# Half-height score products paired across heads, a third pair after half a panel, two weight splits moved and the forget products spread

## The chip, the cores and the metric

The kernel runs on one core of one Trainium2 chip. The metric is the device time of one execution in microseconds (us). The engines are named as the profile names them: PE (TensorE, the matrix products), PEld (its weight loads), DVE (VectorE), ACT (ScalarE), POOL (GpSimd) and SP (SyncE, which issues the DMAs).

## What is computed

The reference takes 256 tokens of width 1024 in fp32 through two stacks.

```python
for l in range(2):                        # first stack
    x = layer_norm(DN_ALPHA * x + 0.5 * swiglu(x, ffn1...))
    x = layer_norm(DN_ALPHA * x + hybrid_mixer(x, ...))
    x = layer_norm(DN_ALPHA * x + 0.5 * swiglu(x, ffn2...))
for l in range(2):                        # second stack
    h = rmsnorm(x);  x = x + merged(attention, convolution, pooling of h) @ w_o
    h = rmsnorm(x);  x = x + (silu(gt) * up) @ w_ffn_out
```

The hybrid mixer has three attentions of 8 heads with 64 channels each: A (a mixture of dilated patterns), B (a band of 128 keys with sinks) and C (64 keys per query, chosen by the score of an indexer with 8 more heads). The second stack has one attention, D, of 8 heads, with a forget gate per token and head: its logits get the difference of running sums of the log of sigmoid(x @ w_f), where w_f has 8 columns.

## The kernel before, in words

**Phases.** The work is a list of phases, `ffn, mix1, ffn` twice and `mix2, ffn` twice. Each engine has its own program that walks this list; the order inside a phase is written out by hand for each engine (`pe_mix1` L1036, `act_mix1` L1178, `pool_mix1` L1264, `dve_mix1` L1376 and the same four for `mix2`), and semaphores join them. Engines work strictly in that order: an instruction that waits holds up all that stands behind it.

**Weights.** They come from HBM in chunks of 128 x 2048 numbers (1 MB). A chunk lands in one of three raw buffers, ACT copies it to `w_hi` rounded to fp32r (`act_split`, L380 to L384), DVE writes the rest to `w_lo` (`dve_split`, L412 to L416), and each product of fp32 numbers is made of three fp32r products (`three`, L419). `act_split` waits until the chunk three places before in the ring has been used, `dve_split` until ACT is done, and the load of a chunk (`sp_chunk`, L364) until the split of the chunk three before it.

**Panels.** In a mixer the input projection is cut into panels of 512 columns. A panel takes two chunks (panel i of the first 13 takes chunks 2i and 2i+1), one for each half of the 1024 input channels. `panel_part` (L917) makes one half for one tile of 128 tokens, 12 products of 512 columns; `panel` makes the four parts, 48 products. Panels alternate between two pairs of PSUM banks, bankA and bankO0/1.

**Small jobs.** Between the panels stand jobs of attention, each in one of four other PSUM banks, taken in turn (`Mixer.small`, `take`, L899): transposes of the rotated queries and keys (`rope`), scores, transposes of the probabilities (`pT`), products with the values (`pv`), transposes of the outputs (`oT`). A job waits until the job four places before it has been read out of its bank (`w_free`).

**Scores.** The 16 score blocks (8 heads by 2 tiles of queries) are made in six units of at most one bank:

```python
UNITS = [(0, (0, 2, 4, 6)), (0, (1, 3, 5, 7)), (1, (0, 2)), (1, (1, 3)), (1, (4, 6)), (1, (5, 7))]
```

The first number is the tile of queries, the second the heads. Even heads lie on partitions 0 to 63 and odd heads on 64 to 127, so that a score product uses the upper or the lower half of the array's rows. A fp32 score product is two entries in the trace (L1060). In `mix2` (L1684 to L1694) each head has a score product (L1691) and one that adds the running sums of the keys (L1693). The units come one after the other, with no other work between. DVE scales, masks and reduces each unit to its row maxima (`logits`, L1443, L1922), ACT takes the exponentials (`exps`, L1134), and PE goes on with `values` (L939): four transposes for each unit, then the products with the values, which wait until ACT has copied the transposed probabilities to `pT` (`p_transposed`, L1152). For the indexer ACT applies a relu to each unit (L1205) into one of two buffers and DVE adds the heads up (`index_sums`, L1398).

**Order around the change.** In `mix1` PE goes: panels 0 to 2 with the transposes of ropes 0 and 1, the first quarter of panel 3, index scores, the rest of panel 3, rope 2, panel 4, rope 3, panel 5, scores B, panel 6, rope 4, values B, panel 7, rope 5, the outputs of B, scores C, panel 8, values C, panel 9, the outputs of C, scores A, panel 10, values A, panel 11. ACT goes, from the indexer on: six relus, the splits of chunks 8 and 9, the copy of panel 3 to `q_raw`, and so on; before values C it has `exps("C")`, the splits of chunks 18 and 19, `gate(8, 1)` and `p_transposed("C")`, and in the same way for A with chunks 22 and 23 and `gate(10, 3)`. POOL makes each rope from `q_raw` in four operations for each tile. In `mix2` PE goes: panels 0 and 1, the transposes of the keys of tile 0, the forget products (`forget_product`, L1613: 32 products of 16 and 8 columns), the keys of tile 1, panel 2, the queries, the running sums, channel panel 3 (96 products of 256 columns), scores D, channel panel 4, panel 5, values D.

Of the kernel before, what the change touches and what calls it, by code (L numbers as in the profile page):

```python
# [98 lines left out]
def build_program(nc, d, out):  # L99
    with ExitStack() as ctx:  # L100
# [10 lines left out]
        A = [bank("bankA0"), bank("bankA1")]  # L111
# [741 lines left out]
        jobs2 = [("qk", 0, 0), ("f",), ("qk", 0, 1)] + [("qk", 1, t) for t in range(TT)] + [("c",), ("cT",)]  # L853
# [49 lines left out]
        def pe_common(pe, M, ph, l, ml):  # L903
# [29 lines left out]

            def panel(i, n=PANEL):
                for h in range(2):
                    for tok in range(TT):
                        panel_part(i, h, tok, n=n)
# [95 lines left out]
            return take, freed, panel, panel_part, values, o_transposes, branch, merged_transposes, out_products  # L1033

        def pe_mix1(pe, ph, l):
            g = G[ph]  # L1036
            M = M1
            (take, freed, panel, panel_part, values, o_transposes, branch, merged_transposes,
# [11 lines left out]
            def scores(kind, n):  # L1050

                for u, (tile, heads) in enumerate(UNITS):
                    b, dst = take((kind, u) if n is None else (kind, n, u))
                    keys = P * (tile + 1)
                    for at, h in enumerate(heads):
                        half = slice(64 * (h % 2), 64 * (h % 2) + 64)
                        q = qi_T if n is None else Q_OF[n]
                        k = {None: kx_T[half, 3, 0:keys], "C": kx_T[half, 2, 0:keys],
                             "B": kx_T[half, h // 4, 0:keys], "A": ka_T[half, h // 2, 0:keys]}[n]
                        mm = pe.matmul(dst[:, at * keys:(at + 1) * keys],  # L1060
                                       q[half, h // 2, tile * P:(tile + 1) * P], k, start=True, stop=True)
                    mm.then_inc(M.w_ready[b], 1)
# [10 lines left out]
            scores("index", None)  # L1073
            panel_part(3, 0, 1)
            panel_part(3, 1, 0)
# [6 lines left out]
            scores("score", "B")  # L1082
            panel(6)
# [5 lines left out]
            scores("score", "C")  # L1089
            panel(8)  # L1090
# [4 lines left out]
            scores("score", "A")  # L1095
            panel(10)
# [83 lines left out]
        def act_mix1(act, ph, l, prefetch):  # L1180
# [19 lines left out]
            for u in range(6):  # L1200
                b, src = ready(("index", u))
# [4 lines left out]
            splits(4)  # L1206
            to_q_raw(3)
            splits(5)
# [1077 lines left out]
```

## Time and profile before

| | |
|---|---|
| median of the runs shown | 2047.75 us (2047.52, 2047.75, 2048.79) |
| the profiled execution, whole | 2049.36 us |
| its span, first to last instruction | 2047.4 us |
| PE busy | 2023.3 us, 99% of the span |
| DVE, ACT, POOL busy | 1233.5, 903.4, 273.3 us |
| mean granted TensorE clock | 0.997 |

The profiled execution lies 1.6 us above the median; 2.0 us of it lie outside the span. A busy PE is not yet a PE at its best: products are pipelined, so the distance between starts, not the length of a product, says how fast they go. Lines such as L421 to L423 are those of `three`; their tiles tell which product it is.

### The profile page before, as it was taken

To read this page: it belongs to the slowest core of one execution; us is meant where nothing else is said; L and a number is where in the kernel's file an instruction comes from. 1 tells how busy PE (TensorE), PEld (TensorE's weight loads), DVE (VectorE), ACT (ScalarE), POOL (GpSimd) and SP (SyncE) were. 2 spreads that over 40 slices of the span, in tenths; PEclk is the share of its full clock that TensorE was granted. 3 is DMA by queue.
4 is the path that set the end of the run, shared out by engine and by line. 5 is a ranking of instruction groups with operands and counts; after the bars stand their busy time and mean duration, and the time that the engine had idled before them with its cause. 6 is when DMAs were issued, how large, how long until landed. Compare 5 with 4: busy or idle time off the path is not lost.

```text
span 2047.4 us, 31170 instructions
## 1 busy us (share of the span) xinstructions
PE 2023.3 (99%) x12476; PEld 1807.8 (88%) x12476; DVE 1233.5 (60%) x1240; ACT 903.4 (44%) x1017; POOL 273.3 (13%) x209
## 2 busy tenths in 40 slices
PE   8999999999999999999999999999999999999999
PEld 7998888889998999878888998898899989888998
DVE  5557685475557555686467557565655566476554
ACT  4444445543444444355543444454444444544442
POOL 0000760010000000651010000323100021240000
PEclk9999999999999999999999999999999999999999
DMA  7655443456565556433365564545565553455553
GB/s 266 198 190 176 134 156 122 167 183 205 184 200 191 185 184 204 161 128 120 128 229 190 185 200 149 172 141 180 169 206 184 187 191 124 163 189 177 186 187 110
DMA packets 249122, 358.33 MB, mean 175 GB/s; under 512 B 24640, under 2 KB 164544, under 8 KB 249024
## 3 DMA queue, kind: packets, MB, share of 16 engines
q1 hardware_dynamic: 248880, 356.85, 53.0%
q8 instruction: 71, 1.16, 0.2%
q14 instruction: 27, 0.22, 0.0%
q10 hardware_dynamic: 144, 0.10, 0.0%
HBM read 355.85 MB, written 1.05 MB: 174 GB/s over the span
## 4 chain that ended last, share of the span: by engine, by line
PE 90%; DVE 5%; ACT 2%; POOL 1%; DMA 1%; issue 1%; SPq 1%; ACTq 0%; DVEq 0%; POOLq 0%
PE bankA L421 16%; PE bankA L423 16%; PE bankA L422 16%; PE bankO L421 12%; PE bankO L422 12%; PE bankO L423 12%; PE bankO L962 1%; DVE w_lo L415 1%; PE bankT L962 1%; PE bankT L447 1%; DVE bias_c L1409 1%; DMA w_raw<-in_w_ffn_in_dram 1%; POOL rope_out L1287 1%; DVE S_sb L1455 1%; DVE nmax L1460 1%
## 5 line engine op out<-in xcount | busy, mean ns | idle before, releaser
L415 DVE TENSOR_TENSOR w_lo<-w_raw,w_hi 128x2048 fp32r<-128x2048 f32 (+2 forms) x297 | 692.2, 2338 | 388.8 <-ACT w_hi L384 388.6
L384 ACT ACTIVATE w_hi<-w_raw 128x2048 fp32r<-128x2048 f32 (+2 forms) x297 | 563.1, 1900 | 458.4 <-PE bankA L423 317.7
L421 PE MATMUL bankA<-xT_hi,w_hi 128*128 128x256 f32 x1888 | 534.7, 283 | 0.0
L423 PE MATMUL bankA<-xT_hi,w_lo 128*128 128x256 f32 x1888 | 534.3, 283 | 0.0
L422 PE MATMUL bankA<-xT_lo,w_hi 128*128 128x256 f32 x1888 | 534.3, 283 | 0.0
L421 PEld LDWEIGHTS bankA<-xT_hi,w_hi 128*128 128x128 f32 x1888 | 362.2, 192 | 3.1 <-issue 0.7
L422 PEld LDWEIGHTS bankA<-xT_lo,w_hi 128*128 128x128 f32 x1888 | 362.2, 192 | 2.4
L423 PEld LDWEIGHTS bankA<-xT_hi,w_lo 128*128 128x128 f32 x1888 | 362.2, 192 | 0.0
L421 PE MATMUL bankO<-w_hi,xT_hi 128*128 128x512 f32 x432 | 173.0, 400 | 1.6 <-DVE w_lo L410 1.5
L423 PE MATMUL bankO<-w_hi,xT_lo 128*128 128x512 f32 x432 | 169.5, 392 | 0.0
L422 PE MATMUL bankO<-w_lo,xT_hi 128*128 128x512 f32 x432 | 169.2, 392 | 0.0
L421 PE MATMUL bankA<-w_hi,xT_hi 128*128 128x512 f32 (+1 forms) x384 | 154.0, 401 | 3.5 <-DVE w_lo L415 2.7
L800 POOL TENSOR_TENSOR rstd<-var_eps,minus_half 128x1 f32<-128x1 f32 x20 | 14.0, 702 | 1047.9 <-DVE var_eps L782 804.1
L423 PE MATMUL bankA<-w_hi,xT_lo 128*128 128x512 f32 (+1 forms) x384 | 150.9, 393 | 0.0
L422 PE MATMUL bankA<-w_lo,xT_hi 128*128 128x512 f32 (+1 forms) x384 | 150.8, 393 | 0.0
L421 PE MATMUL bankO<-w_hi,hT_hi 128*128 128x512 f32 x336 | 131.2, 391 | 0.0
L422 PE MATMUL bankO<-w_lo,hT_hi 128*128 128x512 f32 x336 | 131.2, 391 | 0.0
L423 PE MATMUL bankO<-w_hi,hT_lo 128*128 128x512 f32 x336 | 130.7, 389 | 0.0
L645 ACT ACTIVATE hT_hi<-h_sb 128x512 fp32r<-128x512 f32 x48 | 30.5, 636 | 185.5 <-PE bankO L423 185.5
L421 PEld LDWEIGHTS bankO<-w_hi,xT_hi 128*128 128x128 f32 x432 | 81.7, 189 | 19.9 <-DVE w_lo L410 2.6
L423 PEld LDWEIGHTS bankO<-w_hi,xT_lo 128*128 128x128 f32 x432 | 81.6, 189 | 17.7
L422 PEld LDWEIGHTS bankO<-w_lo,xT_hi 128*128 128x128 f32 x432 | 81.8, 189 | 15.8
(373 smaller groups left out, 3051.5 us busy)
## 6 DMA issues: line engine op xcount, KB each, us to landing
w_raw<-in_w_in_dram SPq DMA_DIRECT2D x184, 512.0 KB, 4.5
w_raw<-in_ffn_in_dram SPq DMA_DIRECT2D x172, 512.0 KB, 4.7
w_raw<-in_ffn_out_dram SPq DMA_DIRECT2D x88, 512.0 KB, 4.2
w_raw<-in_w_ffn_in_dram SPq DMA_DIRECT2D x88, 512.0 KB, 4.7
w_raw<-in_w_ffn_out_dram SPq DMA_DIRECT2D x44, 512.0 KB, 4.2
w_raw<-in_w_out_dram SPq DMA_DIRECT2D x16, 512.0 KB, 4.5
w_raw<-in_w_o_dram SPq DMA_DIRECT2D x16, 512.0 KB, 4.4
w_raw<-in_w_br_b_dram SPq DMA_DIRECT2D x8, 512.0 KB, 4.8
```

What stands on the lines that cost most here:

```text
L384: act.activation(cut(W_HI[slot(ph, i)], n), cut(w_raw[:, i % RING, :], n), ACT.Copy).then_inc(hi_done, 1)
L415: dve.tensor_tensor(cut(W_LO[slot(ph, i)], n), cut(w_raw[:, i % RING, :], n), cut(W_HI[slot(ph, i)], n).bitcast(F32), ALU.subtract).then_i ...
L421: pe.matmul(dst, hi, whi, start=start, stop=False, skip_group_check=True)
L422: pe.matmul(dst, hi, wlo, start=False, stop=False, skip_group_check=True)
L423: return pe.matmul(dst, lo, whi, start=False, stop=stop, skip_group_check=True)
L447: mm = pe.transpose(T[half][:, q * P:(q + 1) * P], buf[:, tok, kt * P:(kt + 1) * P], ident)
L645: act.activation(dst[:], h_sb[:].rearrange("p (t c) -> p t c", t=2), ACT.Copy).then_inc(hT_hi_done, 1)
L962: mm = pe.matmul(dst[:, h * 64:h * 64 + 64], pT[:, c:c + P], v, start=kk == 0, stop=kk == tile)
L1287: pool.tensor_tensor(outs[-1], src, c, ALU.mult).then_inc(rope_step, 1)
L1409: stepped(dve.scalar_tensor_tensor(acc, relu[:, u % 2, at * keys:(at + 1) * keys], misc[:, tile, 448 + h:449 + h], base, ALU.mult, ALU.add))
L1455: dve.scalar_tensor_tensor(s, src.rearrange("p (h k) -> p h k", k=keys), SCALE, m.unsqueeze(1).broadcast_to([P, len(heads), keys]), ALU.mu ...
L1460: red = dve.tensor_reduce(nm, s, AX, ALU.max, negate=True)
```

## The change

The score units are made in pairs, even and odd heads in turn, and the third pair (units 4 and 5) comes after half of the following panel. In `mix1` chunk 8 is split between the second and the third index unit and chunk 9 after the copy of panel 3 (ACT) or of rope 2 (DVE), and chunk 15 is split after `p_transposed("B")` and the copy of `va` (ACT) and after `normalise("B")` (DVE). In `mix2` the forget products are spread over panel 1, one pair behind each three products of 512 columns, and the key transposes come one quarter panel apart.

```diff
@@ PE, mix1
-            def scores(kind, n):
-                for u, (tile, heads) in enumerate(UNITS):
-                    b, dst = take((kind, u) if n is None else (kind, n, u))
...
+            def scores(kind, n, pairs):
+                for first in pairs:
+                    tile, evens = UNITS[first]
                     keys = P * (tile + 1)
+                    pair = [take((kind, u) if n is None else (kind, n, u)) for u in (first, first + 1)]
+                    for at in range(len(evens)):
+                        for parity, (b, dst) in enumerate(pair):
+                            h = evens[at] + parity
...
+                            mm = pe.matmul(dst[:, at * keys:(at + 1) * keys],
+                                           q[half, h // 2, tile * P:(tile + 1) * P], k, start=True, stop=True)
+                            if at == len(evens) - 1:
+                                mm.then_inc(M.w_ready[b], 1)
...
-            scores("index", None)
+            scores("index", None, (0, 2))
             panel_part(3, 0, 1)
+            scores("index", None, (4,))
             panel_part(3, 1, 0)
...
-            scores("score", "B")
-            panel(6)
+            scores("score", "B", (0, 2))
+            panel_half(6, 0)
+            scores("score", "B", (4,))
+            panel_half(6, 1)
...
-            scores("score", "C")
-            panel(8)
+            scores("score", "C", (0, 2))
+            panel_half(8, 0)
+            scores("score", "C", (4,))
+            panel_half(8, 1)
...
-            scores("score", "A")
-            panel(10)
+            scores("score", "A", (0, 2))
+            panel_half(10, 0)
+            scores("score", "A", (4,))
+            panel_half(10, 1)
@@ ACT, mix1
             for u in range(6):
+                if u == 2:
+                    act_split(act, ph, g, 8)
                 b, src = ready(("index", u))
...
-            splits(4)
             to_q_raw(3)
+            act_split(act, ph, g, 9)
             splits(5)
...
             exps("B")
-            act_split(act, ph, g, 15)
             p_transposed("B")
             for tok in range(TT):
                 panel_wait(6, tok)
                 act.activation(va[:, tok, :], A[tok][:, :], ACT.Copy).then_inc(M.m_free[0][tok], 1)
+            act_split(act, ph, g, 15)
@@ DVE, mix1
                 for u, (tile, heads) in enumerate(UNITS):
+                    if u == 2:
+                        dve_split(dve, ph, g, 8)
...
-            splits(4)
             rope_copy(2)
+            dve_split(dve, ph, g, 9)
...
             rope_copy(4)
+            normalise("B")
             dve_split(dve, ph, g, 15)
-            normalise("B")
@@ PE, mix2 (the ticket of job "f" also moves ahead of ("qk", 0, 0))
-            def forget_product():
+            def panel_and_forget(i):
                 b, dst = take(("f",))
                 pe.wait_ge(wf_lo_done, l + 1)
...
+                for h in range(2):
+                    for tok in range(TT):
+                        for t in range(4):
+                            panel_part(i, h, tok, t, 1)
+                            kt, c, tokens = 4 * h + t, 2 * tok * HEADS, slice(tok * P, (tok + 1) * P)
+                            pe.matmul(dst[:, c:c + 2 * HEADS], xT_hi[:, kt, tokens], wf[:, kt, :], ...)
+                            mm = pe.matmul(dst[:, c:c + HEADS], xT_lo[:, kt, tokens], wf[:, kt, 0:HEADS], ...)
...
+            def scores(pairs):
...
+                        for parity, (b, dst) in enumerate(pair):   # both score products, then both of the sums
...
-            panel(1)
+            panel_and_forget(1)
             qk_transposes(0, (0,))
-            forget_product()
+            panel_part(2, 0, 0)
             qk_transposes(0, (1,))
-            panel(2)
+            panel_part(2, 0, 1)
+            panel_half(2, 1)
             qk_transposes(1)
             running_sums()
             channel_panel(3)
             freed(("cT",))
-            scores()
-            channel_panel(4)
+            scores((0, 2))
+            channel_panel(4, (0,))
+            scores((4,))
+            channel_panel(4, (1,))
             panel(5)
```

## Rows read from the trace of the kernel before

**Rows 1.** The page, part 1: busy time, share and count of each engine.

```profile
PE 2023.3 (99%) x12476; PEld 1807.8 (88%) x12476; DVE 1233.5 (60%) x1240; ACT 903.4 (44%) x1017; POOL 273.3 (13%) x209
```

**Rows 2.** The waits of PE: engine, line, releaser, total us, times, longest us.

```profile
PE bankA L421 <- DVE w_lo L415: 2.7, 2, 1.4
PE bankT L962 <- ACT pT L1156: 1.7, 2, 0.9
PE bankO L1047 <- POOL rope_out L1300: 1.3, 2, 0.6
```

**Rows 3.** Windows: busy us of PE, PEld, DVE, ACT, POOL, granted clock, DMA, GB/s.

```profile
1302.00:1306.00 4.00, 4.00 (x36) 4.00 (x33) 2.32 (x5) 1.09 (x2) 3.04 (x3) 0.89 0.80 259
1306.00:1310.00 4.00, 4.00 (x13) 3.41 (x14) 1.47 (x6) 1.22 (x2) 3.84 (x4) 0.50 0.01 2
1310.00:1314.00 4.00, 4.00 (x15) 3.15 (x14) 2.02 (x3) 2.30 (x3) 2.07 (x2) 0.76 0.00 0
```

**Rows 4.** Timeline of PE, forget products: start, us, engine, line, tiles.

```profile
1302.10 0.26 PE L1620 MATMUL bankO<-wf,xT_hi 128*128 128x16 f32 x1
1302.21 0.25 PE L1622 MATMUL bankO<-wf,xT_lo 128*128 128x8 f32 x1
...
1305.55 0.35 PE L1622 MATMUL bankO<-wf,xT_lo 128*128 128x8 f32 x1
1305.76 0.36 PE L1620 MATMUL bankO<-wf,xT_hi 128*128 128x16 f32 x1
```

**Rows 5.** Timeline of PE, scores D of the first mix2.

```profile
1334.09 0.49 PE L1691 MATMUL bankT<-qc_T,qi_T 64*128 64x128 f32 x2
...
1335.53 0.27 PE L1691 MATMUL bankT<-qc_T,qi_T 64*128 64x128 f32 x1
1335.54 0.37 PE L1691 MATMUL bankO<-qc_T,qi_T 64*128 64x128 f32 x1
1335.64 0.27 PE L1691 MATMUL bankT<-qc_T,qi_T 64*128 64x128 f32 x1
...
1341.82 0.38 PE L421 MATMUL bankA<-xT_hi,w_hi 128*128 128x256 f32 x1
```

**Rows 6.** Timeline of PE, from scores C to values C, first mix1.

```profile
314.69 1.37 PE L1060 MATMUL bankT<-kx_T,qc_T 64*128 64x128 f32 x13
...
318.25 1.13 PE L1060 MATMUL bankT<-kx_T,qc_T 64*128 64x256 f32 x4 [0.19 <-DVE S_sb L1455]
319.31 0.50 PE L421 MATMUL bankA<-w_hi,xT_hi 128*128 128x512 f32 x1
...
330.35 1.03 PE L945 MATMUL bankO<-wide,S_sb 128*128 128x128 f32 x8
...
332.22 1.97 PE L962 MATMUL bankO<-misc,pT 128*128 128x64 f32 x16
```

**Rows 7.** Timeline of DVE and ACT in the same stretch.

```profile
321.48 0.68 DVE L1455 SCALAR_TENSOR_TENSOR S_sb<-bankT,bias_c 128x512 f32<-128x512 f32 x1
...
325.23 3.71 ACT L384 ACTIVATE w_hi<-w_raw 128x2048 fp32r<-128x2048 f32 x2
...
330.54 0.60 ACT L1168 ACTIVATE gates<-bankA 128x512 f32<-128x512 f32 x1 [1.13 <-PE bankA L423]
```

**Rows 8.** Timeline of PE and ACT, scores B to values B, first mix1.

```profile
276.48 1.37 PE L1060 MATMUL bankT<-kx_T,qb_T 64*128 64x128 f32 x13
...
292.71 1.90 ACT L384 ACTIVATE w_hi<-w_raw 128x2048 fp32r<-128x2048 f32 x1
...
295.67 1.97 PE L962 MATMUL bankT<-misc,pT 128*128 128x64 f32 x16 [0.85 <-ACT pT L1156]
```

**Rows 9.** Timeline of POOL, rope 3: its first and its last operation.

```profile
252.71 3.33 POOL L1287 TENSOR_TENSOR rope_out<-q_raw,cos 128x512 f32<-128x512 f32 x1 [8.65 <-ACT q_raw L1191]
...
263.59 1.27 POOL L1300 TENSOR_TENSOR rope_out<-rope_out,rope_tmp 128x512 f32<-128x512 f32 x1
```

**Rows 10.** Windows, columns as in rows 3: four us in the first mix2's entry.

```profile
1279.00:1283.00 4.00, 0.56 (x4) 0.14 (x3) 2.51 (x6) 3.18 (x5) 0.55 (x1) 1.00 0.16 10
```

More of the change, by code:

```diff
@@ L1031, in out_products @@
                 next_transposes(pe, ph, 1)
-            return take, freed, panel, panel_part, values, o_transposes, branch, merged_transposes, out_products
+            return take, freed, panel, panel_half, panel_part, values, o_transposes, branch, merged_transposes, out_products
         def pe_mix1(pe, ph, l):
@@ L1037, in pe_mix1 @@
             M = M1
-            (take, freed, panel, panel_part, values, o_transposes, branch, merged_transposes,
+            (take, freed, panel, panel_half, panel_part, values, o_transposes, branch, merged_transposes,
              out_products) = pe_common(pe, M, ph, l, l)
@@ L1600, in pe_mix2 @@
             ml = l + LAYERS
-            (take, freed, panel, panel_part, values, o_transposes, branch, merged_transposes,
+            (take, freed, panel, panel_half, panel_part, values, o_transposes, branch, merged_transposes,
              out_products) = pe_common(pe, M, ph, l, ml)
@@ L1638, in running_sums, with channel_panel @@
                           skip_group_check=True).then_inc(M.w_ready[b], 1)
-            def channel_panel(i):
-                for h in range(2):
+            def channel_panel(i, halves=(0, 1)):
+                for h in halves:
                     pe.wait_ge(lo_done, chunk_no(g, 2 * i + h) + RING)
@@ L1681, in conv_product @@
                         mm.then_inc(*((M.panel_ready, 1) if i == 11 or tok == 0 else (chunk_used, 1)))
-            def scores():
-                for u, (tile, heads) in enumerate(UNITS):
-                    b, dst = take(("score", "D", u))
+            def scores(pairs):
+                for first in pairs:
+                    tile, evens = UNITS[first]
                     keys = P * (tile + 1)
-                    for at, h in enumerate(heads):
-                        half = slice(64 * (h % 2), 64 * (h % 2) + 64)
-                        row = 64 * (h % 2) + h
-                        pe.matmul(dst[:, at * keys:(at + 1) * keys], q2_T[half, h // 2, tile * P:(tile + 1) * P],
-                                  k2_T[half, h // 2, 0:keys], start=True, stop=False)
-                        mm = pe.matmul(dst[:, at * keys:(at + 1) * keys],
-                                       ident[half, row:row + 1].broadcast_to([64, P]), neg_cT[half, 0:keys],
-                                       start=False, stop=True)
-                    mm.then_inc(M.w_ready[b], 1)
+                    pair = [take(("score", "D", u)) for u in (first, first + 1)]
+                    for at in range(len(evens)):
+                        c = slice(at * keys, (at + 1) * keys)
+                        for parity, (b, dst) in enumerate(pair):
+                            half = slice(64 * parity, 64 * parity + 64)
+                            pe.matmul(dst[:, c], q2_T[half, evens[at] // 2, tile * P:(tile + 1) * P],
+                                      k2_T[half, evens[at] // 2, 0:keys], start=True, stop=False)
+                        for parity, (b, dst) in enumerate(pair):
+                            half = slice(64 * parity, 64 * parity + 64)
+                            row = 65 * parity + evens[at]
+                            mm = pe.matmul(dst[:, c], ident[half, row:row + 1].broadcast_to([64, P]),
+                                           neg_cT[half, 0:keys], start=False, stop=True)
+                            if at == len(evens) - 1:
+                                mm.then_inc(M.w_ready[b], 1)
```

31 lines of the change are left out of this document (13 added, 18 removed).

## The prediction, on record before the changed kernel ran

> **What bounds the kernel now.** I read the page first, then the waits of PE, windows of the mixers, and the timeline of each engine around every edit. The page says PE: 2023.3 us busy, 99% of the span, no other engine above 60% [rows 1]. So time can come from three places only: PE's own work made shorter, PE's waits, and PE's clock. The table of waits shows how little stands in the second place, and that what there is belongs to this change [rows 2]: 1.4 us at most on chunk 8's split, twice, 0.9 us twice on ACT before values B, 0.6 us twice on POOL's rope. The windows show the third place [rows 3]: after the forget products the granted clock is 0.50 for the whole of one window and mixed in its neighbours.
>
> The profiled execution took 2049.36 us with a span of 2047.4; the median of the runs is 2047.75. I take gains worked out from the trace off the median. A difference of 0.2%, 4.1 us, is about what can be told from no change.
>
> **The change, part by part, for one layer of each mixer** (the second layer shows the same waits, so all is doubled at the end).
>
> *Forget products.* 32 products of 16 and 8 columns start 0.11 us apart (the first two of [rows 4]): 3.5 us in which PE does nothing wide. At the end of them the clock falls to the lower level, 1.2 GHz: the distance becomes 0.21 us (the last two of [rows 4]). How long it stays down comes from the windows: a mean of 0.89 over 4 us is 0.9 us at half clock, 0.50 is 4.0, 0.76 is 1.9, together 6.8 us [rows 3]. PE was busy throughout, so 3.4 us are lost. Spread, each pair stands behind three products of 512 columns. Its own cost is kept: a small product costs the 0.11 us of its weight load, which nothing 8 columns wide can hide, wherever it stands. So -3.4 us if the clock holds, 0 if it does not; I take -3.4, since PE was never at the lower level beside wide products. The price of the new order: panel 1 ends 3.5 us later, and POOL's work on the queries behind it. I follow that chain through DVE's reduction (now behind the key transpose) and POOL's four us a tile to the query transposes: it arrives within some 0.5 us of PE. I take +0.2, bounds 0 and +1.5.
>
> *Scores D.* From the first score product to the first of panel 4, 7.7 us [rows 5]. Units of unlike parity already overlap where they meet: bankT at 1335.53, bankO at 1335.54, the next bankT at 1335.64 [rows 5]. Two products on the two halves of the rows start 0.01 us apart and neither slows the other. Paired throughout, the first two units take 16 places of 0.11 us, 1.8 us, the others 8 places each of about 0.21 (two times the columns), 1.7 us a pair; with entries and exits between half-height and full-height products, of which there is now one more, 5.9 us. That is -1.8; bounds -0.8 (if PE cannot issue two weight loads and two products in 0.11 us for long; where the overlap shows, it lasts four places) and -1.9. Values D come after two panels, so ACT and DVE have room for the later third pair, and nothing takes it back.
>
> A rule speaks against this part. The Trainium skill (TensorEngine Tiling (Array Packing), Key Properties) says that changing the tiling mode drains the array. The row that bears on it: the last four products of scores C, 256 columns each, take 1.06 us up to the next full-height product [rows 6], where four places of 0.21 are 0.86. So a drain of 0.2 us on the way out, and as much on the way in by my estimate, stands in my sums; the change adds ten such excursions, 4 us in all, already counted.
>
> *Chunk 8.* PE no longer waits for its split, 1.5 us with what the wait's edges cost. But POOL's rope 3 is next. It runs from 252.71 to 264.86 [rows 9], started by ACT's copy of panel 3, and PE waits for it already [rows 2]. In the new order that copy comes when the last relu is done; DVE reaches it 2.3 us later because split 8 stands between its sums, and ACT saves the two splits of 3.7 us. I get the copy 1.05 us earlier, and rope 3 still crosses two DVE splits. So PE's gain, the shorter index scores included, is POOL's, -0.8; bounds -0.3 and -2.0.
>
> *Scores B and chunk 15.* The waits of scores on DVE (0.36 us and its edges) go, and split 15, 1.9 us of ACT ahead of the `pT` copies [rows 8], goes from PE's path. DVE's chain of six units and two splits stays, and then its copy of rope 4, which two of the transposes need. From the start of scores B to the first value product it was 19.2 us (276.48 to 295.67) [rows 8]; by that chain 18.0. So -1.2, bounds 0 and -1.7. Split 15 in its new place ends about 2.5 us before panel 7's second half needs it: nothing.
>
> *Scores C and A.* Here the edit turns against itself. Before, the scores took 4.6 us (314.69 to 319.31) [rows 6], and the value products began 17.5 us after the first score. Now: units 0 to 3 take 2.0 us, the half panel 5.5 (half of 319.31 to 330.35), and the third pair starts at 7.6 and is ready for DVE at 8.75. Before, DVE took unit 4 at 6.8 (321.48) and ACT's splits began at 10.5 (325.23) [rows 7]. All that follows is in ACT's order: exponentials, two splits of 3.7 us, two gate copies and two `pT` copies of about 0.55 us each. Begun 1.95 us later, and no longer waiting for PE (1.13 us [rows 7]), they reach the value products at 18.25. PE, which saved 1.4 us, is there at 15.95 and waits 2.3 us. Net +0.75 for C and the same for A, which has the same rows; bounds -1.4 (no wait at all) and +1.2.
>
> **Sum.** -3.4 + 0.2 - 1.8 - 0.8 - 1.2 + 1.5 = -5.5 a layer, -11.0 us in all: 2047.75 - 11.0 = 2036.8 us.
>
> **The rivals.**
>
> *The clock falls in a new place* (ends slower). The 2.3 us in which PE will stand before values C and A lie between 16 transposes of 1.75 us and small products of 6.2 us (332.22 up to the next panel). Nothing wide runs for ten us. Against it: before values B PE waited 0.85 us in such a stretch [rows 8] and kept its clock, and in the entry of mix2 it was busy 0.56 us in four and kept it [rows 10]. For it: that entry has 512-column products on both sides; the forget products, which did cost the clock, had not even a gap. There are four such places. A fall costs at least the 3.4 us that one costs now; if it covers the value products, each of which doubles as the forget products did (0.11 to 0.21), up to 6.2 us and some 2 more in the panel behind: 3.4 to 8. One fall: 2040 to 2045. Two give 2044 to 2053, three or four up to 2068. It decides from the point where falls cost over 11 us: two long or three short ones. For two or three at 6 us I write 2052.
>
> *The fall at the forget products stays*, because the transposes and the forget work together are still thin: 2043.6. Against it: three wide products to each pair.
>
> *Pairing does not pay*: PE issues too slowly, D gives 0.8 and the index pair nothing more: 2039 to 2041. The Trainium skill (TensorE: Matmul & The Clock Gate, the section on the 56 ns) has about 62 ns of issue for each product; by it a pair of places would take 0.124 instead of 0.11 us, and D would give 1.6 instead of 1.8. The trace cannot tell them apart in four places.
>
> *The waits at C and A do not come*, as ACT's work is quicker than I add up: then these parts give 1.4 each instead of costing 0.75, and the time is 2047.75 - 19.6, about 2028 to 2033.
>
> **How the numbers follow.** The sum as it stands, 2034 to 2040: 0.39, the likeliest. One fall in a new place: 0.14, of which 0.06 below 2043.65. Two or more: 0.32. The old fall stays: 0.04, half of it below. Pairing doesn't pay: 0.05. No waits: 0.06. Faster by over 0.2%: 0.39 + 0.06 + 0.02 + 0.05 + 0.06 = 0.58. Same: 0.10. Slower: 0.32, all of it the clock. Leaving out some 0.15 of the longest falls and a few hundredths of the lowest, the range is 2033 to 2056. Since both signs hold much: the likeliest case alone is 2034 to 2040.
>
> **What would show it.** In the changed profile: granted clock 1.00 through panel 1 and the key transposes of mix2, no row of products 0.21 us apart there; scores D some 5.9 us without the half panel between; no wait on L415 in panel 4 but one of 1 to 2 us on POOL's L1300 before rope 3's second tile; no wait of L1060 on DVE; waits of L962 on ACT's `pT` in C and A of about 2.3 us, four in all, and about 1 us before values B for DVE's copy of rope 4. I am wrong if the windows of values C and A show a clock of 0.5 in more than one place, or if those four waits are missing.

## The result, and the profile after

The changed kernel takes 2065.12 us in the median of four runs (2059.54 to 2066.23); the kernel before took 2047.85 beside it. The ratio is 1.0079, 95% interval 1.0064 to 1.0093: it is 17 us slower. The forecast said 2036.8 with a range up to 2056, so both the sign and the range were wrong. What happened is the first rival: PE's clock fell in new places.

The first two lines of the page (busy times before: [rows 1]):

```profile
span 2064.0 us, 31202 instructions
PE 2028.7 (98%) x12476; PEld 1808.6 (88%) x12476; DVE 1253.3 (61%) x1240; ACT 903.8 (44%) x1017; POOL 270.1 (13%) x209
```

PE has the same 12476 products as before, some of them now side by side, and yet it is busy 5.4 us longer, and the span is 16.6 us longer. So it stands 11.2 us more, and it is slower while it works. The waits of PE (who waited <- for whom: us in total, times, longest us), against [rows 2]:

```profile
PE bankO L965 <- ACT pT L1170: 8.5, 4, 2.1
...
PE bankO L948 <- DVE qi_T L1402: 4.9, 2, 2.7
PE bankA L421 <- DVE w_lo L415: 2.7, 2, 1.4
PE bankO L1066 <- DVE oT_loC L1367: 1.2, 2, 0.6
PE bankO L421 <- DVE w_lo L415: 1.0, 2, 0.5
```

The four waits on `pT` are those the prediction announced, 2.1 us each. The second row was announced as about 1 us and is 2.17 in the first layer and 2.73 in the second. The third stands in panel 4 where chunk 8's wait had been, but it is chunk 9's. The first, second, fourth and fifth row are new, 15.6 us; the 4.5 us that PE waited before values B, between the scores and for POOL are gone. That leaves the 11 us of standstill. The rest of the loss is clock. Windows of 4 us through values B and values A of the first layer (columns as in [rows 3]: busy us and count of PE, PEld, DVE, ACT, POOL, then the granted clock, DMA share and GB/s):

```profile
292.00:296.00 4.00, 1.83 (x16) 1.42 (x14) 3.97 (x6) 2.26 (x8) 3.92 (x5) 0.98 0.17 66
296.00:300.00 4.00, 4.00 (x20) 4.00 (x20) 0.90 (x3) 0.53 (x1) 3.77 (x4) 0.50 0.00 0
300.00:304.00 4.00, 4.00 (x22) 4.00 (x20) 0.23 (x2) 3.70 (x5) 0.00 (x0) 0.50 0.02 4
...
308.00:312.00 4.00, 4.00 (x16) 3.23 (x15) 4.00 (x3) 0.00 (x0) 0.00 (x0) 0.81 0.12 10
374.00:378.00 4.00, 1.88 (x17) 1.67 (x16) 4.00 (x2) 4.00 (x7) 0.00 (x0) 0.97 0.17 24
378.00:382.00 4.00, 4.00 (x21) 4.00 (x21) 0.75 (x3) 0.56 (x2) 0.00 (x0) 0.50 1.03 373
382.00:386.00 4.00, 4.00 (x27) 4.00 (x26) 0.54 (x2) 2.99 (x3) 0.00 (x0) 0.68 0.36 134
```

In both places a window in which PE was busy for 1.8 or 1.9 us of four comes first, and then PE, fully busy, runs at 0.50, that is at 1.2 GHz. The timeline of PE at values B shows the stop and what it costs behind it:

```profile
294.64 1.25 PE L948 MATMUL bankO<-wide,S_sb 128*128 128x128 f32 x8 [2.17 <-DVE qi_T L1402]
295.73 3.42 PE L965 MATMUL bankT<-misc,pT 128*128 128x64 f32 x16
298.95 1.06 PE L948 MATMUL bankT<-wide,S_sb 128*128 128x128 f32 x4
```

The first 16 products with the values (`pT` in the row) took 1.8 us up to the next transposes before (295.67 to 297.47); here they take 3.2 (295.73 to 298.95). Such falls lie at values B and A in the first layer, at values C and A in the second, and one more at the entry of the first mix2, where PE waits 3.48 us for `hn`; their sum is 44.4 us at half clock, so 22 us lost, against 6.8 before (13.7 us at half clock, both times at the forget products).

Stage by stage, from starts of products in the two traces (us, first and second layer, "after" in the same order; "pv" is the first product with the values; a forecast is for one layer):

| stage | before | forecast | after |
|---|---|---|---|
| index scores to scores B | 37.89, 37.85 | -0.8 | 37.72, 37.64 |
| scores B to pv B | 19.19, 19.19 | -1.2 | 19.42, 19.98 |
| pv B to scores C | 19.03, 19.03 | 0 | 25.71, 19.19 |
| scores C to pv C | 17.52, 17.51 | +0.75 | 18.89, 18.90 |
| pv C to scores A | 18.14, 18.14 | 0 | 18.15, 24.65 |
| scores A to pv A | 17.56, 17.56 | +0.75 | 19.20, 19.22 |
| pv A, first to last | 6.09, 6.10 | 0 | 9.36, 7.74 |
| mix2, entry to next phase | 196.2, 193.4 | -5.0 | 194.1, 187.8 |

The differences add up to 17.3 us, against 16.6 between the two spans; the other phases together took 0.7 us less. 18.1 of them are the four falls in the mixers (6.7, 6.5, 3.3 and 1.6 in the rows 3, 5 and 7 of the table), 6.9 are mix1 without the falls (the forecast for it was -1.0), and mix2, its entry's fall included, gave back 7.7.

What was forecast of mix2 came. A window over panel 1 with the forget products in it:

```profile
1318.00:1322.00 4.00, 4.00 (x24) 3.40 (x23) 2.42 (x5) 2.89 (x3) 3.20 (x3) 1.00 1.04 380
```

And scores D, against [rows 5]: PE's timeline at the start of the first two pairs, at the start of the third pair, and at the first panel product behind each.

```profile
1358.04 0.37 PE L1713 MATMUL bankT<-qc_T,qi_T 64*128 64x128 f32 x1
1358.05 0.37 PE L1713 MATMUL bankO<-qc_T,qi_T 64*128 64x128 f32 x1
...
1358.48 0.27 PE L1718 MATMUL bankT<-kx_T,wide 64*128 64x128 f32 x1
1358.49 0.27 PE L1718 MATMUL bankO<-kx_T,wide 64*128 64x128 f32 x1
1358.59 0.27 PE L1713 MATMUL bankT<-qc_T,qi_T 64*128 64x128 f32 x1
1358.60 0.27 PE L1713 MATMUL bankO<-qc_T,qi_T 64*128 64x128 f32 x1
...
1361.76 0.39 PE L421 MATMUL bankA<-xT_hi,w_hi 128*128 128x256 f32 x1
```
```profile
1367.70 0.48 PE L1713 MATMUL bankT<-qc_T,qi_T 64*128 64x256 f32 x1
...
1369.62 0.39 PE L421 MATMUL bankA<-xT_hi,w_hi 128*128 128x256 f32 x1
```

3.72 and 1.92 us, 5.64 together (forecast 5.9, before 7.73). Behind the first pair, which takes 0.21 us, two products of 128 columns share each 0.11 us all the way, so "pairing does not pay" is out. The Trainium skill (TensorE: Matmul & The Clock Gate, "Wait — 56ns, not 53.3ns?") has the 62 ns for each product only where hardware decode is off, a condition that the prediction left out; no run here shows which decode was at work. By that figure two products would have needed 0.124 us, and the trace has 0.11.

Why was the stop at values B so long? DVE's timeline of the changed kernel in the first layer, and POOL's beside it:

```profile
291.43 0.42 DVE L1455 TENSOR_SCALAR bias_c<-bias_c 128x128 f32<-128x128 f32 x2
291.77 2.22 DVE L1459 TENSOR_TENSOR bias_c<-bias_c,wide 128x128 f32<-128x128 f32 x2
293.91 1.27 DVE L1402 COPY qi_T<-bankO 128x512 f32<-128x512 f32 x2
```
```profile
291.64 1.33 POOL L1303 TENSOR_TENSOR rope_out<-q_raw,cos 128x512 f32<-128x512 f32 x1 [17.14 <-PE bankO L1050]
292.94 0.77 POOL L1307 TENSOR_TENSOR rope_tmp<-q_raw,sin 128x256 f32<-128x256 f32 x1
```

The same two additions of `chosen` (DVE's step that makes the mask of C) took 0.62 us in the kernel before:

```profile
291.93 0.62 DVE L1441 TENSOR_TENSOR bias_c<-bias_c,wide 128x128 f32<-128x128 f32 x2
```

POOL's rope 5 waits for PE's transposes of rope 4. PE reached them 1.5 us earlier (290.57 instead of 292.03) while DVE's chain hardly moved, and so POOL's first operations met DVE's additions. The copy of rope 4 stands behind them and the transposes of units 2 and 3 behind that. In the second layer it was a smaller one that they met: DVE's addition of 8 columns to `sinkm` (L1489, at 934.70) took 1.27 us instead of 0.17, beside POOL's first operation of 1.28 us (at 934.67), and the steps of `chosen` behind it were stretched too. The Trainium skill (SBUF — State Buffer, SBUF: two separate sides) says that a DVE operation with two SBUF inputs and a POOL operation that reads SBUF exclude each other for a whole instruction. The trace agrees: the first of the two additions took 1.36 us instead of 0.29 and ended at 293.13, behind the POOL operation that ended at 292.97, and the second took 0.94 instead of 0.42 beside POOL's next one of 0.77.

### The profile page after: what moved, and what is told of

Same layout as the page of the kernel before. It is cut to its first block, busy times and chain, and to the rows that moved or that the text cites. A ratio compares the mean times of both kernels' runs of the same rounds, so it can differ in the third digit from the quotient of the medians.

```text
span 2064.0 us, 31202 instructions
## 1 busy us (share of the span) xinstructions
PE 2028.7 (98%) x12476; PEld 1808.6 (88%) x12476; DVE 1253.3 (61%) x1240; ACT 903.8 (44%) x1017; POOL 270.1 (13%) x209
## 4 chain that ended last, share of the span: by engine, by line
PE 90%; DVE 6%; ACT 2%; issue 1%; DMA 1%; SPq 0%; POOL 0%; DVEq 0%; ACTq 0%
PE bankA L421 16%; PE bankA L423 16%; PE bankA L422 16%; PE bankO L421 12%; PE bankO L422 12%; PE bankO L423 12%; DVE w_lo L415 2%; PE bankO L965 2%; PE bankT L965 1%; DVE bias_c L1427 1%; PE bankT L447 1%; ACT w_hi L384 1%; DVE nmax L1478 1%; DMA w_raw<-in_w_ffn_in_dram 1%; DVE S_sb L1473 1%
## 5 line engine op out<-in xcount | busy, mean ns | idle before, releaser
L421 PE MATMUL bankO<-w_hi,xT_hi 128*128 128x512 f32 x432 | 177.2, 410 | 1.9 <-DVE w_lo L415 1.0
L423 PEld LDWEIGHTS bankO<-w_hi,xT_lo 128*128 128x128 f32 x432 | 82.3, 190 | 18.1
```

The lines of the kernel that those rows point to most:

```text
L421: pe.matmul(dst, hi, whi, start=start, stop=False, skip_group_check=True)
L423: return pe.matmul(dst, lo, whi, start=False, stop=stop, skip_group_check=True)
```

## The experiments

Twelve kernels ran, each beside the kernel before on the same chip; a ratio is that of its time to that kernel's. Diffs are against the changed kernel, but for e8 to e10 (against the kernel before) and e11, e12 (against e7). A fall below is a stretch of granted clock 0.50 among the value products.

**e1: whole panels for B, C and A.**

```diff
-            scores("score", "C", (0, 2))
-            panel_half(8, 0)
-            scores("score", "C", (4,))
-            panel_half(8, 1)
+            scores("score", "C", (0, 2, 4))
+            panel(8)
```

and the same for B (panel 6) and A (panel 10).

> The changed kernel with the third pair of units of B, C and A back beside the other two and the whole panel behind them; the alternation of parities, the moved splits and the spread forget products stay. Theory (the half panel delays ACT and DVE, PE then stands still among transposes and value products, and there the clock falls): the four waits of 2.12 us on pT go, no window of values A, B or C shows a clock of 0.5, and the time is 2047.85 - 6.8 (forget) - 3.6 (scores D) - 1.6 (chunk 8) - 1 to 3 (scores) = 2033 to 2035, or up to 3.4 more if the entry of mix2 still loses its clock. Rival 1 (the alternating score products themselves, denser and with more changes between half and full height, cost the clock): the falls stay, 2052 to 2062. Rival 2 (the falls are a matter of where each stretch happens to lie): some stay at other places, 2038 to 2050.

2037.74 us, ratio 0.9956 (0.9942 to 0.9970). No stop among the values and no fall there; the theory holds, and rival 1 (the alternation) is out. PE waits for DVE at the third pair instead:

```profile
PE bankT L1066 <- DVE S_sb L1467: 6.2, 6, 1.5
```

The entry of mix2 still lost its clock, which the expectation put at up to 3.4 us more.

**e2: whole panels for C and A only.** The e1 edit without B.

> Only C and A have their third pair back beside the others. Theory: the waits on pT go and with them the falls at values C and A, 23.9 us of half clock in the profiled run of the changed kernel, so 12 us, while the 1.4 us that the scores had gained by the half panel go back against the 2.1 us of each wait (-0.7 each, -2.8): 2065.1 - 12 - 2.8 = 2050. The fall at values B (13.65 us of half clock, 6.8 us) stays. Rival 1 (alternating products cost the clock): no change of the falls, about 2062. Rival 2 (placement): B's stretch of layer 2 may now fall as well, 2050 to 2057.

2048.43 us, ratio 1.0005 (0.9994 to 1.0017), near the theory's 2050: no wait on `pT`, no fall at C or A, the stops at B (2.17 and 2.73 us) as they were, with a fall in the first layer only in the profiled execution.

**e3: a whole panel for B only.** The e1 edit for B alone.

> Only B has its third pair back beside the others. Theory: DVE gets units 4 and 5 before the panel, its chain to the copy of rope 4 ends earlier, the 2.17 us stop of PE inside the transposes of values B goes and with it its fall (6.8 us): 2065.1 - 6.8 - 1 = 2057, the falls at C and A as before. Rival 1 (alternating products): 2064. Rival 3 (the stop comes from POOL's rope 5 beside DVE's chosen, whatever the scores do): the stop stays at 1.5 to 2.2 us and so does the fall, 2064.

2054.47 us, ratio 1.0039 (1.0023 to 1.0056): the stop at B is gone. Rival 3 had the collision right, but not "whatever the scores do": with the whole panel ahead of the transposes of rope 4, PE reaches them at 291.94 instead of 290.57, POOL starts at 293.02, and DVE's additions are through by then.

```profile
291.76 0.62 DVE L1457 TENSOR_TENSOR bias_c<-bias_c,wide 128x128 f32<-128x128 f32 x2
293.02 1.28 POOL L1301 TENSOR_TENSOR rope_out<-q_raw,cos 128x512 f32<-128x512 f32 x1 [18.50 <-PE bankO L1050]
```

The C and A stops were all there (8.5 us in four), yet in the profiled execution only those of the second layer cost the clock. Windows around values C of both layers, the same work at the same pace:

```profile
328.00:336.00 8.00, 5.88 (x50) 5.47 (x49) 5.41 (x5) 6.43 (x10) 0.00 (x0) 1.00 0.45 148
961.00:969.00 8.00, 5.88 (x43) 5.52 (x42) 5.41 (x5) 5.84 (x9) 0.00 (x0) 0.89 0.49 163
```

PE is busy 5.88 of 8 us in both; one keeps the clock and one doesn't. The twelve runs of this kernel reach from 2046.6 to 2068.2: whether a stop costs the clock is settled anew each time.

**e4: pT ahead of both splits.**

```diff
             exps("C")
+            p_transposed("C")
             splits(9)
             gate(8, 1)
-            p_transposed("C")
```

and the same for A.

> The half panels stay everywhere; ACT copies pT of C and of A before the splits of chunks 18, 19 and 22, 23 and the gates, not after them. Theory (it is the standstill that costs the clock): PE no longer waits 2.12 us four times (-8.5), the falls at C and A go (-12), the later splits are in time for panels 9 and 11: 2044 to 2046, with B's fall still there. Rival 4 (a long stretch without wide products costs the clock even without a gap): the waits go, the falls stay, 2056. Rival 5 (the splits become late instead): waits of L421 on w_lo in panels 9 and 11, 1 to 3 us each.

2058.18 us, ratio 1.0041 (1.0026 to 1.0057): far above the theory's 2045. The standstill was not taken away but moved, four times 1.34 us. Without a stop among the values, PE stops for the late split behind them:

```profile
342.85 0.59 PE L421 MATMUL bankO<-w_hi,xT_hi 128*128 128x512 f32 x1 [1.34 <-DVE w_lo L415]
```

```profile
342.00:346.00 4.00, 3.15 (x8) 2.47 (x9) 3.93 (x6) 3.03 (x4) 0.00 (x0) 0.64 0.51 140
```

Rival 5 came as written (1.34 us, four times), and in the first layer both of these stops came with a fall of 3.4 us. The other part of the miss is at values B: here the second layer fell too, for 17.1 us, where the changed kernel's profiled execution had kept its clock at the same stop. The experiment left open whether thin products alone would do (rival 4). e5 settles that.

**e5: one split on each side of pT.**

```diff
             exps("C")
-            splits(9)
-            gate(8, 1)
+            act_split(act, ph, g, 18)
             p_transposed("C")
+            act_split(act, ph, g, 19)
+            gate(8, 1)
```

and the same for A with chunks 22 and 23.

> The changed kernel; before values C and A ACT does only one of the two splits (18, 22) ahead of the copies of pT, the other split (19, 23) and the gate copies behind them. Theory (a standstill of PE, wherever it comes beside products of 64 columns, costs the clock; moving both splits behind, as before, only moved the standstill of 1.3 us to panels 9 and 11): ACT's exponentials end at 334.7 and one split takes 1.9 us, so pT is in time, and chunk 18 and 19 are in time for panel 9; no wait over 0.5 us at C and A, no fall there, 2065.1 - 8.5 - 12 = 2044 to 2047 with B's falls and the entry of mix2 left. Rival (thin products alone cost it): the falls at the end of values C and A stay, 3.4 us of half clock each as with both splits behind, 2048 to 2055.

2045.67 us, ratio 0.9993 (0.9982 to 1.0004). The waits on `pT` and the late splits at C and A are gone, and with them every fall there, though the row of thin products is as long as before. The falls at B remain, in both layers of the profiled execution (297 and 928 us). So this row of narrow products (some 8 us of transposes and value products) keeps the clock when nothing stops it.

**e6: copy of rope 4 ahead of the mask.**

```diff
+            rope_copy(4)
             chosen()
-            rope_copy(4)
```

> The changed kernel; DVE copies rope 4 before it makes the choice mask of C, not after it. Theory: the stop of PE inside the transposes of values B (2.17 and 2.7 us) goes, because it was the mask under POOL's rope 5 that was late and not the half panel, and B's fall goes with it: 2065.1 - 4.9 - 6.8 = 2053 to 2055; the four waits on pT and the falls at C and A stay. Rival: the stop becomes a wait on something behind the copy (the sinks' sums, ACT's pT) of 1 us or more and the fall stays, 2060 to 2064.

2054.09 us, ratio 1.0035 (1.0020 to 1.0051). The stops at B shrink to 0.28 and 0.79 us, and B keeps its clock; all four stops at C and A are followed by falls in the profiled execution.

**e7: all mends.** The edits of e5 and e6, and

```diff
-            rope_copy(2)
             dve_split(dve, ph, g, 9)
+            rope_copy(2)
```

> Both of these together, and chunk 9's DVE split before the copy of rope 2. Half panels, alternation, moved splits and spread forget products all stay. Theory: no stop over 1 us is left between the products of B, C and A, no fall but perhaps one at the entry of mix2: 2065.1 - 8.5 - 12 - 4.9 - 6.8 - 1.5 = 2031 to 2035, below the version with whole panels by what the scores' waits on DVE cost there (6.2 us). Rival (half panels thin the stretch by themselves): falls stay, 2037 to 2045, and whole panels are the better way.

2033.58 us (2031.45 to 2035.78), ratio 0.9938 (0.9924 to 0.9951): the theory's range, and faster than both kernels. Half panels, alternation, moved splits and spread forget products are all in it. Its busy times, three of its waits (that on POOL is the longest left in mix1) and two windows, over values B and values A:

```profile
PE 2009.8 (99%) x12476; PEld 1790.4 (88%) x12476; DVE 1253.1 (62%) x1240; ACT 903.3 (44%) x1017; POOL 270.0 (13%) x209
```
```profile
PE bankO L1050 <- POOL rope_out L1318: 2.0, 2, 1.0
PE bankO L1066 <- DVE oT_loC L1369: 1.2, 2, 0.6
PE bankO L948 <- DVE qi_T L1404: 0.8, 1, 0.8
```
```profile
296.00:300.00 4.00, 4.00 (x39) 4.00 (x38) 1.74 (x5) 3.48 (x5) 3.92 (x5) 1.00 0.01 4
...
368.00:372.00 4.00, 4.00 (x36) 3.92 (x35) 1.48 (x1) 4.00 (x6) 0.00 (x0) 1.00 0.60 224
```

**e8: the stop alone, in the kernel before.** ACT makes two copies into `q_raw`, which nobody reads any more in that layer, ahead of the copies of `pT` of C and of A.

```diff
+            act.wait_ge(rope_done, (l + 1) * (ROPES * TT))
+            for at in range(2):
+                act.activation(q_raw.rearrange("p t (r c) -> p (t r) c", r=4), ident.unsqueeze(1).broadcast_to([P, 8, P]), ACT.Copy).then_inc(dose_step, 1)
+                act.wait_ge(dose_step, 4 * l + 0 + at + 1)
             p_transposed("C")
```

and the same for A, with `4 * l + 2 + at + 1`.

> The kernel before, with two needless copies of 1024 columns on ACT (into a free buffer) ahead of the copies of pT of C and of A, about 1.0 us each: a standstill of PE of some 2 us at the same four places, but between two whole panels, with nothing else changed. Theory (the standstill costs the clock): 2047.85 + 4 x 2.1 = 2056 and falls at one to four of the places, 3.4 to 6.8 us of half clock each, 2058 to 2066. Rival (the standstill costs only itself; the half panel with the third pair in it, or the alternation, is needed for a fall): four waits of 2 us, no new fall, 2055 to 2057.

2062.73 us (2058.09 to 2068.81), ratio 1.0079 (1.0061 to 1.0096): the changed kernel's ratio, from the kernel before and four stops. The wait, and the clock behind three of the four:

```profile
333.62 1.97 PE L963 MATMUL bankO<-misc,pT 128*128 128x64 f32 x16 [2.14 <-ACT pT L1157]
```
```profile
338.00:342.00 4.00, 4.00 (x21) 4.00 (x20) 0.00 (x0) 1.52 (x1) 0.00 (x0) 0.50 0.00 0
...
380.00:384.00 4.00, 4.00 (x22) 4.00 (x20) 0.80 (x2) 2.99 (x3) 0.00 (x0) 0.50 0.01 2
...
980.00:984.00 4.00, 4.00 (x25) 4.00 (x25) 0.80 (x2) 1.22 (x3) 0.00 (x0) 0.60 0.50 178
```

Neither half panel nor alternation is needed. Four stops of 2.14 us are 8.6 us, and the kernel lost 15.5 (2047.24 beside it): the stop costs itself and, three times in four here, the clock.

**e9: only the forget products spread** (the whole `panel_and_forget` part of the change).

> The kernel before with only the forget products spread over panel 1 and the key transposes one quarter panel apart. Theory: the two falls of 6.8 us of half clock go, -3.4 each, and the new order costs nothing to see: 2047.5 - 6.8 = 2040 to 2041, with no product of the mixers at the lower clock. Rival: the chain of the queries behind the later panel 1 makes PE wait 1 us or more a layer, or the entry of mix2, which has lost its clock in every version with the changed mix1 and in none with the old one, loses it here too: 2042 to 2044.

2044.65 us, ratio 0.9986 (0.9977 to 0.9995), 3.2 us faster and not 6.8. The second mix2 gives the full sum: 193.4 us become 189.9. In the first, 196.2 became only 195.4: the fall at the forget products is gone, but the entry lost its clock here, which in the profiled execution of before it had kept [rows 10].

```profile
1279.00:1283.00 4.00, 0.53 (x3) 0.23 (x2) 2.51 (x5) 3.18 (x5) 0.55 (x1) 0.97 0.16 11
1283.00:1287.00 4.00, 4.00 (x16) 3.31 (x16) 1.07 (x2) 0.75 (x2) 0.00 (x0) 0.60 0.63 172
```

Nothing of the change lies ahead of that entry in this kernel, so its loss is no effect of mix1, although every version with the changed mix1 had lost it.

**e10: only scores D changed.**

> The kernel before with only scores D changed (alternation, third pair after half of channel panel 4). In the changed kernel the scores took 5.64 us against 7.73, so theory: -2.1 a layer, 2047.5 - 4.2 = 2043. Rival (the time gained there is lost again in a wait behind it, for values D): 2045 to 2047.5, with a new wait of L945 or L962 in mix2.

2044.15 us, ratio 0.9981 (0.9972 to 0.9990), the theory's 2043 to 1.2 us; no new wait before values D. In the profiled execution the entry of the first mix2 lost its clock here too.

**e11: the mended kernel with whole panels** (e7 with the edit of e1).

> The version with all mends (one split ahead of pT, copy of rope 4 first, chunk 9 ahead of the copy of rope 2), but with the third pair of B, C and A back beside the others and whole panels. Theory: with the falls gone the half panel is worth what the scores otherwise wait for DVE, 1.5 us at B and 0.8 at C and A (the waits of the version with whole panels), 3.1 a layer less 0.5 to 1 of waits that it causes before the values: 2033.6 + 4 to 6 = 2038 to 2040. Rival (the half panel never paid, and the mends carry the whole gain): 2033 to 2035.

2037.83 us, ratio 0.9954 (0.9940 to 0.9968), against 0.9938 of e7. The waits of the third pair on DVE are back at 6.2 us. The first mix1, from its first transposes to those of the next phase, takes 250.0 us here and 247.9 in e7, the second 249.8 and 248.3: the half panel is worth 2.1 and 1.5 us once it causes no stop.

**e12: the mended kernel without alternation.**

```diff
-                    pair = [take(("score", "D", u)) for u in (first, first + 1)]
-                    for at in range(len(evens)):
...
+                    for parity in range(2):
+                        b, dst = take(("score", "D", first + parity))
...
+                        for at in range(len(evens)):
```

and in the same way in mix1.

> The version with all mends, half panels kept, but the two units of a pair made one after the other everywhere, as before. Theory: alternation is worth 2.1 us a layer in D and some 0.4 in the index scores and up to 1.1, 0.4 and 0.4 in B, C and A, as far as the waits on DVE between the pairs don't swallow it: 2033.6 + 4.2 + 2 to 4.6 = 2040 to 2042. Rival (only D gains, as elsewhere DVE sets the pace): 2037.5 to 2039.

2039.89 us, ratio 0.9964 (0.9950 to 0.9978). The time lies between the theory's and the rival's, and the mechanism is the rival's: mix1 takes 248.1 and 248.3 us against 247.9 and 248.3 in e7, so there alternation is worth 0.2 us or nothing. Scores D carry the difference of 6.3 us between the two kernels: the first two pairs take 5.79 us and the third 2.90, against 3.72 and 1.92, so 3.05 in each of two layers.

```profile
1325.50 0.37 PE L1715 MATMUL bankT<-qc_T,qi_T 64*128 64x128 f32 x1
...
1331.29 0.38 PE L421 MATMUL bankA<-xT_hi,w_hi 128*128 128x256 f32 x1
...
1337.23 0.48 PE L1715 MATMUL bankT<-qc_T,qi_T 64*128 64x256 f32 x1
...
1340.13 0.39 PE L421 MATMUL bankA<-xT_hi,w_hi 128*128 128x256 f32 x1
```

8.69 us, while undivided and unalternated scores took 7.73, so dividing them costs 1.0 us. Nearly all of it is overlap: where units 3 and 4 met, in the kernel before, the last four products of the one and the first four of the other took 0.98 us side by side (1338.92 to 1339.90); divided, they take 0.96 (1330.33 to 1331.29) and 0.97 (1337.23 to 1338.20) one after the other.

```profile
1338.92 0.70 PE L1691 MATMUL bankT<-qc_T,qi_T 64*128 64x256 f32 x4
1339.90 0.38 PE L1691 MATMUL bankT<-qc_T,qi_T 64*128 64x256 f32 x1
```

**All profiled executions together.** There are 84 value stretches (B, C, A in two layers of 14 kernels, before and after included). The fall begins in the last 0.7 us of the stop or up to 2.2 us behind it:

| stop of PE in or right behind the stretch | stretches | with a fall |
|---|---|---|
| none, or up to 0.88 us | 56 | 0 |
| 1.34 us, behind it | 4 | 2 |
| 2.1 to 2.7 us, in it | 24 | 18 |

The entry of the first mix2, with its stop of 3.4 us, lost the clock in 12 of the 14, the second, which has no such stop, in none. Other stops of 0.9 us and more, all of them shorter than 2 us, never came with a fall: 22 of 1.31 to 1.38 us in panel 4 of mix1, between products of 512 columns; 6 of 1.52 us between score products, with a panel on both sides (e1, e3, e11); 6 of 0.95 to 1.06 us in the transposes of rope 3; 8 of 0.90 to 1.73 us at the entries of the phases behind mix2.

## Why the prediction was wrong

**The step that failed is the price of the stops before values C and A.** The sum has them as waits alone, "Net +0.75 for C and the same for A", and puts the clock at nothing; it went into a rival with a chance of 0.46. The waits came, at 2.12 us against 2.3 forecast. What the runs showed in place of "nothing" is that a stop of 2.1 to 2.7 us there comes with a fall in 18 of 24 stretches, and that the four falls in the mixers cost 18.1 us of the changed kernel. By that rate "no fall" at four such stops was the least likely outcome, and not the likeliest. The evidence set against it was a stop of 0.85 us before values B and a half-idle window at the entry of mix2. The first belongs to a class that never cost the clock (0 of 56, ten of them with a stop of 0.79 to 0.88 us), so it said nothing about stops of over 2 us. The second was one execution of an entry that loses its clock in 12 of 14. A row that "kept its clock" is one draw. The rival's own arithmetic was sound: "three or four up to 2068" holds what came, but the likeliest value was written down as 2052, and the range was cut at 2056, below the price worked out.

One reading of the rows leaned the wrong way as well: "PE was never at the lower level beside wide products". The fall of [rows 3] goes on beside them: the first products of 512 columns behind the forget products start 0.43 us apart (1307.52 and 1307.95 in the kernel before), against 0.23 at full clock. It began among narrow ones, and that much was right.

From the forecast to the result it is 28 us. Of these 18.1 are the four falls in the mixers, 3.4 the fall at the entry of the first mix2, 3.4 scores B, 3.1 scores C and A, and 1.2 chunk 8; the rest of mix2 gave 1.1 more than forecast.

**Scores B and chunk 15** was the second failure: -1.2 forecast, +0.2 and +0.8 measured, and it made a fifth and a sixth stop of over 2 us. "DVE's chain ... stays, and then its copy of rope 4" left out that the earlier transposes also release POOL, beside which the last pieces of that chain are stretched: the two additions took 2.22 us instead of 0.62. I had looked at what DVE waits for and not at what PE's gain would start. With the copy moved ahead (e6) the stage takes 17.4 and 18.0 us, the 18.0 forecast.

**Scores C and A**: +0.75 forecast, +1.4 and +1.65 measured. The waits were right to 0.2 us; I missed that the second pair now waits for DVE's copies out of the banks (0.34 us at C, 0.62 at A), so that the third pair started 8.2 us behind the first score instead of 7.6 (329.67 less 321.44), and 8.5 at A.

**Chunk 8**: -0.8 forecast, -0.2 measured. The wait on its split went, but the wait on POOL that I expected in its place did not come, because chunk 9's split, now beside rope 3, took 3.02 us and held PE 1.38 us; chunk 11's held it 0.5 us later. With split 9 ahead of the copy of rope 2 (e7) the stage gives 0.8 and 0.9 us, and the wait on POOL of 1.0 us appears as forecast.

**The forget products** were right: -3.6 us in the second mix2 against -3.4 + 0.2, no fall beside the wide products, no late query. **Scores D** were mis-sized by 0.3 us on the safe side, 5.64 for 5.9. The term is the passage between full and half height, 0.2 us each way in the sum. The changed kernel's rows give about 0.1 in (the first step is 0.21 us instead of 0.11, and 0.32 instead of 0.21 in the third pair) and 0.1 out (0.30 from 1369.32 to the panel, instead of 0.21).

**The whole**: with the stops mended the kernel takes 2033.6 us, ratio 0.9938, near the 2036.8 of the forecast. That nearness confirms little: e7 has three edits that the forecast kernel lacks, and it is the case of the prediction's last rival, no waits at C and A, for which it had 2028 to 2033. What stands is the price of the forget products and, within 0.3 us, of scores D; the parts of mix1 had waits left out, and the rival taken for a possible mishap decided the case.

## What to carry to other kernels

A long stop of PE is not priced by its length. Here one of 2.1 to 2.7 us among narrow products cost its length and, three times in four, the clock on top, up to 7.6 us of it (values B of e5, second layer: 46.8 us from scores B to scores C, where the changed kernel with the same stop and no fall took 39.2). One of 3.4 us between wide products cost the clock in 12 of 14. Stops under 0.9 us never did, and of those between 0.9 and 2 us only the ones right behind the value products (2 of 4). So before moving work, count the stops of 2 us and more that it creates, and those of over a microsecond beside narrow products, and take each as a likely fall; one clean pass in one trace is no proof against it. When PE comes earlier somewhere, follow also what its semaphores start on POOL, and move the copy that PE needs next ahead of whatever collides with it.

## What the runs showed of the hardware

- The same kernel keeps or loses the clock from one execution to the next at the same place with the same stop (e3's values C in the two layers; runs of e3 from 2046.6 to 2068.2 us), and the version without long value stops has a narrow spread (e7, five runs: 2031.45 to 2035.78). The kernel before, without them too, spread from 2043.8 to 2053.2 in 21 runs, so a wide spread alone does not point at them.
- The length of a fall varies as much: 3.4 to 17.1 us at half clock for a stop among the value products (3.4 for values A of the changed kernel's second layer, 13.7 for its values B), 3.4 or 6.8 at the entry of the first mix2, between products of 512 columns.
- Products of 128 columns on the two halves of the rows start in pairs every 0.11 us for 30 products on end (scores D, behind a first pair of 0.21 us), and those of 256 columns every 0.21 or 0.22, so the two halves do work side by side for as long as the program alternates.
- Divided scores without alternation cost 1.0 us more than undivided ones, but 0.86 of it (four places of 0.215 us) is the lost overlap of two units. An extra passage from full to half height and back is thus left with 0.1 to 0.2 us by this estimate; the starts of the changed kernel's scores D give 0.1 in and 0.1 out.
- DVE's operations with two inputs in SBUF and POOL's operations stretch one another: two additions of 0.62 us became 2.22, one of 0.17 became 1.27, a split that took 2.28 us ten microseconds earlier, with POOL idle, took 3.02, and POOL's operation beside that split took 3.35 us instead of 1.30.

Three things stay open. What decides, at a given stop of 2 us, whether the clock falls was not settled: it varies between executions. A stop of 1 to 2 us inside a value stretch was not tried, so the table has nothing between 0.88 and 2.1 us there. And no stop of 2.1 to 2.7 us was put between wide products, so whether the narrow ones around it are needed at that length is not shown. The counts are from one profiled execution of each kernel.
